# Normed rows transposed among the last output groups, four low parts on VectorE, loads spaced by merges

## The reference

```python
mod = silu(c) @ ada_w + ada_b ;  sh1, sc1, g1, sh2, sc2, g2 = split(mod, 6)
h = rms_norm(x, norm1_w) * (1 + sc1) + sh1
z = h @ w_in                       # retention q,k,v,gate; attention q,k,v,forget; two branch gates gr, gf
merged = sigmoid(gr) * (y_ret @ ret_proj) + sigmoid(gf) * (y_fox @ fox_proj)
x = x + g1 * (merged @ w_out)      # the "final projection"
h2 = rms_norm(x, norm2_w) * (1 + sc2) + sh2
x = x + g2 * ((silu(h2 @ w_gate) * (h2 @ w_up)) @ w_down)      # w_gate, w_up: 1024 x 2816
return rms_norm(x, norm_f_w)
```

## Time and profile before

| | us |
|---|---|
| median of 3 runs (lowest, highest) | 1936.36 (1935.87, 1937.72) |
| profiled execution, its time | 1936.59 |
| its span in the trace | 1934.8 |
| PE busy in the span | 1853.2 (96%) |
| DVE, ACT, POOL busy | 1115.0, 681.7, 1004.2 |

### The profile page before, as it was taken

How to read it: one execution, slowest core, us unless ns; L and a number is a source line. 1 busy time by engine, 2 the same in 40 slices (tenths; PEclk the granted TensorE clock), 3 DMA queues, 4 the chain that set the end, 5 groups by cost and what they waited for, 6 DMA issues and landing times.

```text
span 1934.8 us, 24236 instructions
## 1 busy us (share of the span) xinstructions
PE 1853.2 (96%) x8634; PEld 1536.4 (79%) x8634; DVE 1115.0 (58%) x1649; ACT 681.7 (35%) x1222; POOL 1004.2 (52%) x615
## 2 busy tenths in 40 slices
PE   4989999999999999999999997989999999999998
PEld 3778778888888778878888886877888888878887
DVE  6834764455554566766565547674455555555636
ACT  5633240323223333223332231174444434442123
POOL 1776642435261677775536346249888878800000
PEclk8999998999999999999999998999999999999999
DMA  8056631112021544434222124612444434399864
GB/s 328 33 174 193 231 100 35 45 28 61 23 55 25 188 151 158 168 104 161 70 76 70 43 79 181 238 68 67 146 158 153 163 134 159 122 379 364 302 222 172
DMA packets 186530, 272.18 MB, mean 141 GB/s; under 512 B 10281, under 2 KB 122825, under 8 KB 186193
## 3 DMA queue, kind: packets, MB, share of 16 engines
q1 hardware_dynamic: 176466, 243.20, 37.3%
q10 hardware_dynamic: 9984, 27.91, 4.0%
HBM read 194.23 MB, written 76.85 MB: 140 GB/s over the span
## 4 chain that ended last, share of the span: by engine, by line
PE 80%; DVE 5%; DMA 5%; POOL 4%; issue 3%; ACT 2%; SPq 0%; ACTq 0%; DVEq 0%; POOLq 0%
PE ps L1188 43%; PE ps L1655 10%; PE ps L1656 10%; PE ps L1657 10%; PE ps L1578 2%; PE ps L1267 1%; PE ps L1269 1%; PE ps L1268 1%; DMA b_da<-f_units 1%; POOL b_a_wu L979 1%; DMA b_mix<-ret_merge 1%; DMA ret_merge<-b_macc 1%; POOL b_a_raw L983 1%; DVE b_ada_acc L2523 1%; ACT b_act_q L2231 0%
## 5 line engine op out<-in xcount | busy, mean ns | idle before, releaser
L1188 PE MATMUL ps<-b_hT,b_w_split 128*128 128x512 f32 x2528 | 631.1, 398 | 3.7 <-POOL b_w_split L970 2.0
L1188 PEld LDWEIGHTS ps<-b_hT,b_w_split 128*128 128x128 f32 x2528 | 463.9, 190 | 93.7 <-DVE b_rm L2402 2.2
L1655 PE MATMUL ps<-b_act_q,b_wu 128*128 128x512 f32 x616 | 240.3, 390 | 9.0 <-DVE b_act_q L2402 4.6
L1657 PE MATMUL ps<-b_act_q,b_wu 128*128 128x512 f32 x616 | 239.8, 389 | 0.0
L1656 PE MATMUL ps<-b_act_q,b_wu 128*128 128x512 f32 x616 | 239.6, 389 | 0.0
L967 POOL TENSOR_TENSOR b_spare<-b_w_stage 1x1 f32<-1x1 f32 x66 | 21.7, 328 | 416.3 <-PE ps L1188 329.4
L1150 POOL TENSOR_TENSOR b_wu<-b_raw,b_wu 128x512 fp32r<-128x512 f32 x110 | 165.5, 1514 | 57.0 <-ACT b_wu L2207 56.8
L968 POOL TENSOR_SCALAR b_w_split<-b_w_stage 128x1024 fp32r<-128x1024 f32 x66 | 182.6, 2766 | 0.0
L2402 DVE TENSOR_TENSOR b_macc<-ps,b_macc 128x512 f32<-128x512 f32 x188 | 122.6, 687 | 79.9 <-PE ps L1269 49.6
L970 POOL TENSOR_TENSOR b_w_split<-b_w_stage,b_w_split 128x1024 fp32r<-128x1024 f32 x66 | 161.5, 2447 | 5.5
L1655 PEld LDWEIGHTS ps<-b_act_q,b_wu 128*128 128x128 f32 x616 | 115.6, 188 | 35.2 <-issue 10.1
(11 more groups left out here) (285 smaller groups left out, 3443.6 us busy)
## 6 DMA issues: line engine op xcount, KB each, us to landing
f_units<-b_fu SPq DMA_DIRECT2D x70, 512.0 KB, 2.6
b_w_stage<-in_w_in SPq DMA_DIRECT2D x53, 512.0 KB, 4.0
down_units_d<-b_wd SPq DMA_DIRECT2D x66, 256.0 KB, 2.0
b_da<-f_units SPq DMA_DIRECT2D x11, 1536.0 KB, 6.4
b_macc<-in_ada_w SPq DMA_DIRECT2D x32, 512.0 KB, 4.5
b_dr<-down_units_d SPq DMA_DIRECT2D x14, 1024.0 KB, 9.8
b_da<-f_units SPq DMA_DIRECT2D x7, 2048.0 KB, 8.0
b_wd<-in_w_down SPq DMA_DIRECT2D x11, 1024.0 KB, 5.0
```

Source lines behind the costliest of these rows:

```text
L1188: return pe.matmul(o, l, r, start=start, stop=stop)
L1655: pe.matmul(o, l[0], r[0], start=begin and at == 0, stop=False, skip_group_check=go_on)
L1657: return pe.matmul(o, l[1], r[0], start=False, stop=at == end, skip_group_check=go_on)
```

## The change

The first four normed row blocks are turned inside the last output groups: 16 transposes between groups (6,1) and (7,0), 16 between (7,0) and (7,1). The second four follow unit 3 and unit 7. To make room, activation units 0 to 3 no longer have buffers of their own but lie in W_out's tiles (`act_pair`), of which one column half is free after (7,0). The low parts of W_out tiles 4 to 7 are made by DVE after merges 3, 4, 6 and 7 (`LOW_AT`), ACT makes the high parts after merges 1, 3, 5 and 6 (`HIGH_AT`) and each merged block's high part ahead of the next load's two issues. x's blocks are loaded after merges 5, 6, 8 and 10. DVE modulates channel blocks 4 to 7 of the second row half instead of ACT, and row block 7 is normed last. Loads of the down projection's first three units wait for units 2, 5 and 6 of the last pair instead of 1, 3 and 5; in the first stage the raw tiles of pair 3 are loaded right behind those of pair 2.

```diff
-        act_q = [None] * Q7
-        for q, kb in enumerate((64, 80, 168, 184, 40, 136, 152)):
+        act_q = {}
+        for q, kb in ((4, 168), (5, 40), (6, 152)):
...
+        def act_pair(u, hl, kp):
+            if u in act_q:
+                return act_q[u][:, hl, 2 * kp:2 * kp + 2, :]
+            cols = slice((0, HALF, HALF, 0)[u], (0, HALF, HALF, 0)[u] + HALF)
+            if u < 2:
+                return w_split[:, 2 * kp:2 * kp + 2, hl, cols]
+            return (wo_ab, wo_de)[kp][:, 0:2, hl, cols]
+        def act_k(u, hl, k):
+            return act_pair(u, hl, k // 2)[:, k % 2, :]
+        def turn_bank(th, d):
+            return d % 4 if th == 0 else (4, 5, 6, 1, 2, 4, 5, 6)[d]
...
             if g < 3:
-                eng.wait_ge(u_used, AFTER_QK + Q7 * (FT - 1) + 2 * g + 1)
+                eng.wait_ge(u_used, AFTER_QK + Q7 * (FT - 1) + (2, 5, 6)[g])
...
+        HIGH_AT = {1: 4, 3: 5, 5: 6, 6: 7}
+        LOW_AT = {3: 4, 4: 5, 6: 6, 7: 7}
...
                 if b == 2:
                     a_raw_load(2)
+                    a_raw_load(3)
                 for p in range(2):
                     park(p, b)
-                if b == 1:
-                    a_raw_load(3)
...
-            sp.wait_ge(m_sum, MERGE_AT[KT - 1, 1] + 1)
-            sp.dma_start(resid[:, 0:2, :], x_v[:, 0:2, :]).then_inc(s_xagain, 16)
+
+            def resid_load(i, merges):
+
+                sp.wait_ge(m_sum, merges)
+                sp.dma_start(resid[:, 2 * i:2 * i + 2, :], x_v[:, 2 * i:2 * i + 2, :]).then_inc(s_xagain, 16)
+
+            resid_load(0, MERGE_AT[KT - 1, 1] + 1)
             wo_load(7)
             for i in range(1, 4):
-                sp.dma_start(resid[:, 2 * i:2 * i + 2, :], x_v[:, 2 * i:2 * i + 2, :]).then_inc(s_xagain, 16)
+                resid_load(i, MERGE_AT[KT - 1, 1] + 2 * i)
...
-            wo_scale(4)
-            for i in range(5, KT):
+            for i in range(4, KT):
                 wo_scale(i)
-                wo_low(i - 1)
-            wo_low(KT - 1)
             def gate_up_units(p, parts=(0, 1)):
...
+            def row_transposes(th, d):
+
+                bank = turn_bank(th, d)
+                if th == 0:
+                    if d == 0:
+                        pe.wait_ge(n_xn, TT + 2)
+                        pe.wait_ge(n_xp, 2)
+                        pe.wait_ge(o_acc, 12)
+                    elif d >= 4:
+                        pe.wait_ge(h_mdd, AFTER_QK + d - 3)
+                else:
+                    if d == 0:
+                        pe.wait_ge(n_xn, TT + TT - len(POOL_ROWS))
+                        pe.wait_ge(n_xp, len(POOL_ROWS))
+                        pe.wait_ge(o_acc, 16)
+                        pe.wait_ge(h_mdd, AFTER_QK + KT)
+                    elif d > 4:
+                        pe.wait_ge(h_mda, AFTER_QK + d - 4)
+                for b in range(4):
+                    last = pe.transpose(ps[:, bank, blk(b)], macc[:, 4 * th + b, blk(d)], ident)
+                last.then_inc(h_tr, 1)
+
             for t in range(6, 8):
                 for q in range(2):
                     pe.wait_ge(o_acc, 2 * (t - 4) + q + 1)
                     for i in range(KT):
                         last = wo_part(i, t, q)
                     last.then_inc(o_pj, 1)
+                    if (t, q) in ((6, 1), (7, 0)):
+                        for d in range(4):
+                            row_transposes(0, d if t == 6 else d + 4)
...
-            for d in range(KT):
-                row_transposes(0, d)
-            for d in range(4):
-                row_transposes(1, d)
+            pe.wait_ge(h_mdd, AFTER_QK + 5)
             for n in UNIT_RUN:
                 u = n % Q7
                 pe.wait_ge(u_rdy, AFTER_QK + n + 1)
                 pe.wait_ge(h_lo, h_op(u, 1))
-                if n == Q7:
-                    pe.wait_ge(h_mda, AFTER_QK + KT)
                 for k in range(KT // 2):
-                    if n == 0 and k == KT // 4:
-                        for d in range(4, KT):
-                            row_transposes(1, d)
                     last = gate_up_part(n, n, u, k)
                 last.then_inc(u_used, 1)
+                if n in (3, Q7):
+                    for d in range(4):
+                        row_transposes(1, d if n == 3 else d + 4)
...
-                act.wait_ge(m_sum, m + 1)
+                merged_hi(m)
                 if m in after:
                     mix_load(after[m])
-                merged_hi(m)
-                if m in (0, 2, 4, 7):
-                    wo_high({0: 4, 2: 5, 4: 6, 7: 7}[m])
+                if m in HIGH_AT:
+                    wo_high(HIGH_AT[m])
...
-            norm_rows(1, resid, macc, lambda t: act.wait_ge(o_acc, 2 * t + 2), skip=POOL_ROWS)
+            for t in range(TT - 1):
+                row_square(t)
+                if t > 0:
+                    row_root(t - 1)
+                if t >= 2 and t - 2 not in POOL_ROWS:
+                    row_scaled(t - 2)
+            row_root(6)
...
+                if u == 0:
+                    act.wait_ge(o_pj, 15)
...
             unit_hi(0)
+            row_scaled(6)
+            unit_hi(3)
+            row_square(7)
+            row_root(7)
+            row_scaled(7)
             for d in range(4):
                 mod_block(d)
-            unit_hi(3)
+            unit_hi(1)
+            unit_hi(5)
+            act.wait_ge(s_mid, 16 * TT)
+            unit_hi(4)
             weight_hi(8)
             weight_hi(9)
-            for d in range(4, KT):
-                mod_block(d)
-            act.wait_ge(s_mid, 16 * TT)
-            for u in (1, 5, 4, 2, 6):
-                unit_hi(u)
+            unit_hi(2)
+            unit_hi(6)
...
-                    act.wait_ge(u_used, AFTER_QK + Q7 * (FT - 1) + 2 * g + 2)
+                    act.wait_ge(u_used, AFTER_QK + Q7 * (FT - 1) + (2, 4, 4)[g])
...
+            def wo_low(i):
+
+                dve.wait_ge(o_hi, i + 1)
+                lo(wo_home(i)[:, 1, :], w_stage[:, (T_WO + i) % 2, :], wo_home(i)[:, 0, :]).then_inc(o_rdy, 1)
+
             for m in range(11):
                 merge(m)
+                if m in LOW_AT:
+                    wo_low(LOW_AT[m])
...
-            for t in range(4, TT):
+            for t in range(4, 7):
...
-            for d in range(KT):
-                if d in (2, 4):
-                    norm_steps(1, TT + d // 2 - 1)
-                mod_block(d)
...
+            for d in range(4):
+                mod_block(0, d)
+            mean(1, 6)
+            inverse(1, 5)
+            add_out(14)
+            for d in range(4, KT):
+                mod_block(0, d)
+            inverse(1, 6)
+            unit_low(0)
+            add_out(15)
+            unit_low(3)
+            mean(1, 7)
+            inverse(1, 7)
+            block_sums(1)
+            for d in range(4, KT):
+                mod_block(1, d)
+            unit_low(1)
+            block_sums(4)
+            unit_low(5)
+            block_sums(2)
+            unit_low(4)
+            block_sums(6)
+            unit_low(2)
+            unit_low(6)
```

More of the change, by code:

```diff
@@ L1661, in gate_up_part @@
                 return passes(ps[:, bank, :], (w[:, 0, blk(k)], w[:, 1, blk(k)]),
[L1662 to L1690 removed]
+                              (act_k(u, 0, k), act_k(u, 1, k)), k, KT // 2 - 1, begin)
+            pe.wait_ge(h_mdd, AFTER_QK + 5)
             for n in UNIT_RUN:
@@ L2211, in _, with row_square, row_root, row_scaled @@
             act.wait_ge(m_lo, AFTER_HC + len(MERGES))
-            norm_rows(1, resid, macc, lambda t: act.wait_ge(o_acc, 2 * t + 2), skip=POOL_ROWS)
+            def row_square(t):
+                act.wait_ge(o_acc, 2 * t + 2)
+                act.activation(macc[:, t, :], resid[:, t, :], ACT.Square, accum_out=stat[:, 0, t:t + 1]).then_inc(n_sq, 1)
+            def row_root(t):
+                act.wait_ge(n_ms, TT + t + 1)
+                act.activation(stat[:, 2, t:t + 1], stat[:, 1, t:t + 1], ACT.Sqrt).then_inc(n_rt, 1)
+            def row_scaled(t):
+                act.wait_ge(n_r, TT + t + 1)
+                act.activation(macc[:, t, :], resid[:, t, :], ACT.Copy, scale=stat[:, 3, t:t + 1]).then_inc(n_xn, 1)
+            for t in range(TT - 1):
[5 more added lines that the diff above has]
+            row_root(6)
             act.wait_ge(s_amul, 2)
@@ L2887, in _, with mod_block @@
             dve.wait_ge(s_amul, 2)
[L2889 to L2892 removed]
+            def mod_block(th, d):
+                dve.wait_ge(h_tr, AFTER_QK + d + 1 + (0 if th == 0 else KT))
+                dve.tensor_scalar(macc[:, 4 * th:4 * th + 4, d * P:(d + 1) * P],
+                                  ps[:, turn_bank(th, d), :].rearrange("p (b c) -> p b c", c=P),
                                   amul[:, d:d + 1], modT[:, 3 * KT + d:3 * KT + d + 1], ALU.mult, ALU.add).then_inc(h_mdd, 1)
[L2895 to L2898 removed]
             def block_sums(u):
@@ L2916, in block_sums, with unit_low @@
```

(2 more changed lines are left out.)

41 lines of the change are left out of this document (4 added, 37 removed).

## The result

| | before | changed |
|---|---|---|
| median of 5 runs (lowest, highest), us | 1936.79 (1935.87, 1938.92) | 1946.29 (1940.73, 1947.77) |
| ratio to before, 95% interval | | 1.0041 (1.0027 to 1.0055) |
| profiled execution, its span | 1936.59, 1934.8 | 1946.93, 1945.1 |

The account below looks back on a forecast made before the run. PE holds 80% of the chain that ended last, so its idle and slow stretches decide. -4.5 (first half) + 16.8 (wait on POOL) - 0.4 (turn) + 0 = +11.9 on 1936.59: 1948 us forecast, range 1940 to 1953.

Parts of the forecast that it names:

- POOL's wait: Before the first row transposes: PE waits about 11 us for POOL's scaled rows; +16.8 us to the last group's end.
- Rival 1: At the first row transposes: no wait on POOL's rows comes and the change gains, about 1933 us; chance 0.09.
- rival 2: First half of the projection gains 9 to 12 us, paying half or more of the wait; 1937 to 1942; chance 0.10.
- Size of the first half: Final projection's first half: last merge summed at about 1240 instead of 1244.5, -4.5 us, bounds -2 and -9.5.
- I take the 7.0 us of such a landing: Before the fifth group: merge 6's load, issued with x's first block, lands after 7.0 us, at 1198.9.
- One gap of under 5 us: First half of the projection: PE's gaps of 3.45 and 3.90 us shrink to one of under 5.
- Rival 3: First half gains nothing, since x's last block holds the eight additions; net +15 to +18, 1953; chance 0.10.
- The rule on VectorE and GpSimd: Two-SBUF-input VectorE and SBUF-reading GpSimd instructions exclude each other; moved low parts hold POOL up to 1.2 us each, harmlessly.
- The turn: From last output group to the eighth unit: DVE bounds it, about as long as before; -0.4 us, bounds -4 and +3.
- First stage: Gate pair 3's raw tiles loaded earlier: PE's 5.92 us wait on ACT stays; 0, bounds -0.4 and +1.5.
- Down projection: Later activation loads change nothing, as the 2 MB load ahead sets the second unit's landing; 0, bounds -3 and +5.4.
- Sum: Whole kernel: -4.5 + 16.8 - 0.4 + 0 = +11.9 us on the profiled execution.

Follow-up runs that it names:

- turn alone: The changed kernel with the first half of the final projection put back as before the change; 1950.41 us, 1.0077 of the kernel before.
- Squares first: The changed kernel with ACT's norm of rows 0 to 5 ahead of its weight high parts, DVE's inverses likewise early, POOL's list untouched; 1952.29 us, ratio 1.0081 to before.
- rows first: As squares first, but POOL also scales row blocks 1 and 3 ahead of its weight sums and low parts, 5 behind; 1933.50 us, ratio 0.9984 to before.
- x late: Rows first, second-half modulations alternating between ACT and DVE, W_out's last tile loaded before x, x's blocks after merges 7, 8, 11, 11; 1928.79 us, 0.9960 of before.
- spacing alone: The kernel before with only x's four block loads spaced by merges; 1939.45 us, ratio 1.0016 to before.
- down loads alone: The kernel before with only the down projection's first three activation loads issued later (units 2, 5, 6); 1935.45 us, ratio 0.9994 to before.

## Why the prediction was right, and where it was not

- **POOL's wait: right in place, size and price, short in its reason.** 11.1 us measured for "about 11", on the engine and line named, with half the clock behind it. The turn alone shows that nothing else is needed. From the wait's end to Q it took 16.5 us for 16.8. The reason given, the sums and low parts ahead of POOL's rows, is half of it: ACT's norm stands behind the same weight work and was as late (inverse of row 3 at 1267.8, POOL free at 1267.9). Squares first and rows first show that POOL's order costs 18.8 us once ACT is early. Rival 1 (no wait) is out; rival 2 (9 to 12 us from the first half) too.
- **Size of the first half: the term was mis-sized.** Forecast -4.5, measured -2.7 for the last merge counted from the first group (and 1.0 more that belongs to this execution's earlier start, as the spread of starts shows). The step that failed is "I take the 7.0 us of such a landing": it was 9.2. So PE started the fifth group 32.6 us after the first instead of 29.9; 2.2 us of this are the landing and 1.1 the low part (4.2 us from the landing on, where the sum had 3.1, since POOL's last scaling did hold an operation for 2.83 us), while the load went out 0.7 us sooner than reckoned. The block of x and the tile of W_out (512 KB) are no difference: before, both went within 0.4 us of this load, with three more blocks behind them. What was new is that the tile before, issued 2.8 us ahead of this load, was still under way until 1192.1, and that the last tile came 0.8 us behind the load. No run moves these alone; what the block of x itself costs is 4.4 us (9.5 against 5.1, x late). The fourth group did end as said (1195.1 for 1196.1, with a start 1.0 earlier).
- **One gap of under 5 us: wrong.** It was 8.63. My own numbers gave 5.9 (1202 less 1196.1), and the line on what would show it should have said so. Its cost in clock was right in kind, but no fixed price: the group behind the gap of 3.45 us took 8.23 us before, and behind the same gap 7.05 with spacing alone and 5.69 in the turn alone.
- **Low parts and spacing.** I had put both into one term and the hope on the spacing. Apart, the low parts with ACT's new order carry all of it (-4.9 at the last merge), the spacing takes 2.2 of that back in these traces (1.2 by the medians, which the intervals do not tell from nothing). Rival 3 was right in its mechanism (x's last block holds the additions: 4.33 us of waiting at 1223.9) and wrong in its extent.
- **The rule on VectorE and GpSimd** of the Trainium skill (SBUF — State Buffer, "Who interferes with whom") held in both directions. The moved low parts of the change met no operation of POOL, so they held nothing. In rows first, where DVE's low parts of unit 0 fell beside POOL's weight work, two of them took 3.59 us instead of 2.34, and POOL's operation beside them 2.30 instead of 1.28:

```profile
1268.64 3.59 DVE L2460 TENSOR_TENSOR b_w_split<-b_macc,b_w_split 128x1024 fp32r<-128x1024 f32 x2
```

```profile
1268.86 2.30 POOL L1170 TENSOR_TENSOR b_wu<-b_raw,b_wu 128x512 fp32r<-128x512 f32 x1
```

- **The turn: right,** 35.9 us for 36.1, with a DVE wait of 4.61 us for row 7's way, and waits on DVE's low parts further on. Before it had been 36.5. (In the steps, eight pairs follow the four modulations, not ten; the 33.0 is worked out with eight.)
- **First stage: right at 0.** PE's wait there is 5.68 us instead of 5.92, on ACT; with the old order of loads it was 5.78 to 5.96 in five other traces, with the new one 5.71 to 5.96 in six. It was not run alone.
- **Down projection: 0 forecast, -1.6 measured,** inside the bounds (-3 to +5.4), through the clock and not through the load. The premise held: the second unit's load landed 5.8 us behind the 2 MB load ahead of it before, after and with the down loads alone. But that one itself landed sooner, in 18.3 us instead of 21.2, and so the second unit's in 16.3 instead of 22.1, issued 2.8 us later behind the first one; PE waited 2.74 for it instead of 3.32.
- **Sum.** +11.9 forecast, +10.3 in the profiled execution: the first half 1.8 too much, less the start's 1.0, the down projection and what lies ahead of it 2.0, the other terms within 0.4. The errors partly cancelled: that the sum came within 1.6 us is in part luck, that the wait costs 16.6 us where 16.8 was reckoned is not. The prediction gives its range twice, as +6 to +15 and as 1940 to 1953 (+4 to +17); the two do not match, and +9.5 lies in both.

## What to carry to other kernels

Work that is pulled forward on the engine that bounds takes its inputs' deadline along: look at which engines deliver them, what stands ahead of them in each of those lists, and move them there too, or the pulled work turns its old cover into a wait (here 12.8 us between the changed kernel and the one with the norm early on both ACT and POOL). A releaser in the profile is only the last of those that were late: look how close the next one is (here 0.1 us). When moving a list's head, look who feeds it: norm work ahead of ACT's high parts cost POOL 6 us where POOL's own order was not changed with it. Spacing transfers helped here only once it moved the one that collides with the load that somebody waits for; and a landing time read in one pattern of issues (7.0 us) did not hold in the next (9.2), though the transfers were the same.

## What was not expected of the hardware

- A wait of 2.4 to 2.7 us of PE was followed by a full granted clock in three traces and by 0.95 to 0.96 over 35 us in three others, at a cost of 1.6 us.
- ACT scales a row block of 128x1024 in 1.13 to 1.15 us, POOL takes 2.85 for the same, and 4.87 beside DVE's low parts (row 5 in rows first). The first square root on ACT is preceded by a table load of 1.28 us, which the norm's way to the first inverse contains.
- The time at which the final projection starts differs by 4.3 us between traces of kernels whose code ahead of it is the same, more than most single edits here are worth; points of a trace are best compared as distances within it.
